# Fifteen output rows of three tiles moved into the last attention body of a streaming encoder layer

## The reference

```
shift, scale, gate = split(silu(c) @ w_ada + b_ada)
h = x * (1 + scale) + shift
qa, ka, va, ga, qb, kb, vb, gb, qi, ki, wi = split(h @ w_in)
oa = banded window attention with sinks and relative bias    (16 heads, 2 key heads)
ob = attention over the top-k keys of an indexer              (16 heads, 2 key heads)
y  = concat(oa * silu(ga), ob * silu(gb)) @ w_out             (2048 x 2048)
x  = LayerNorm(ALPHA * x + gate * y) * ln_g + ln_b
```

## Time and profile before

| | us |
|---|---|
| median of 3 runs | 2007.69 (2005.69 to 2008.35) |
| profiled execution | 2006.17 |
| its span | 2004.4 |
| TensorE busy | 1911.7 (95%) |
| DVE busy | 973.0 (49%) |
| ACT busy | 704.3 (35%) |
| POOL busy | 618.4 (31%) |

### The profile page before, as it was taken

One profiled execution on the slowest core, in us unless ns is written; L12 is line 12 of the kernel. 1 busy time (PEld: TensorE's weight loads), 2 busy tenths in 40 slices (PEclk: granted clock), 3 DMA queues, 4 the chain that ended last, 5 costly groups with the idle time before them and its releaser, 6 DMA issues.

```text
span 2004.4 us, 34267 instructions
## 1 busy us (share of the span) xinstructions
PE 1911.7 (95%) x13047; PEld 1580.4 (79%) x13047; DVE 973.0 (49%) x2360; ACT 704.3 (35%) x1541; POOL 618.4 (31%) x688
## 2 busy tenths in 40 slices
PE   6799999999999999999999999999999889999994
PEld 3367779888888888888888888888887568878773
DVE  2442448856767778874323323323234522226437
ACT  2224332113433343333443434434435622212221
POOL 0331111112222222222333333333323544434552
PEclk8799999999999999999999999999999999999997
DMA  9964112332332332222211111111125154453564
GB/s 342 342 219 137 33 27 69 98 77 75 81 81 63 84 83 77 68 75 64 62 27 44 43 28 44 27 44 44 27 56 174 49 141 133 127 157 116 181 160 121
DMA packets 251267, 195.43 MB, mean 97 GB/s; under 512 B 149969, under 2 KB 203473, under 8 KB 249313
## 3 DMA queue, kind: packets, MB, share of 16 engines
q1 hardware_dynamic: 216560, 160.26, 28.4%
q10 hardware_dynamic: 33472, 28.75, 4.6%
q0 software_dynamic: 1072, 4.24, 0.7%
HBM read 172.86 MB, written 24.53 MB: 98 GB/s over the span
## 4 chain that ended last, share of the span: by engine, by line
PE 83%; DMA 5%; DVE 3%; ACT 3%; POOL 2%; SPq 2%; issue 2%; ACTq 0%; POOLq 0%; DVEq 0%
PE psum L1729 13%; PE psum L1731 12%; PE psum L1730 12%; PE psum L1765 6%; PE psum L1789 6%; PE psum L1809 5%; PE psum L1833 4%; PE psum L1834 4%; PE psum L1835 4%; PE psum L1656 3%; DMA w_raw<-in_w_out_dram 3%; PE psum L1658 3%; PE psum L1657 3%; DMA ada_ring<-in_w_ada_dram 2%; PE psum L1700 2%
## 5 line engine op out<-in xcount | busy, mean ns | idle before, releaser
L1729 PE MATMUL psum<-h_hi,w_hi 128*128 128x364 f32 (+1 forms) x1536 | 521.5, 340 | 5.4 <-issue 3.6
L1731 PE MATMUL psum<-h_lo,w_hi 128*128 128x364 f32 (+1 forms) x1536 | 503.9, 328 | 0.0
L1730 PE MATMUL psum<-h_hi,w_lo 128*128 128x364 f32 (+1 forms) x1536 | 501.8, 327 | 0.0
L1205 POOL TENSOR_TENSOR w_lo<-w_raw,w_hi 128x512 fp32r<-128x512 f32 x128 | 165.1, 1290 | 494.7 <-ACT w_hi L989 494.7
L1729 PEld LDWEIGHTS psum<-h_hi,w_hi 128*128 128x128 f32 x1536 | 289.2, 188 | 14.5 <-issue 11.2
L1730 PEld LDWEIGHTS psum<-h_hi,w_lo 128*128 128x128 f32 x1536 | 289.7, 189 | 0.0
L1731 PEld LDWEIGHTS psum<-h_lo,w_hi 128*128 128x128 f32 x1536 | 288.5, 188 | 0.0
L1043 ACT ACTIVATE w_raw<-psum 128x512 f32<-128x512 f32 (+1 forms) x176 | 95.9, 545 | 497.8 <-PE psum L1789 497.6
L1219 POOL TENSOR_SCALAR room<-room 128x256 f32<-128x256 f32 (+6 forms) x312 | 166.0, 538 | 320.1 <-DVE room L1439 318.1
L1211 POOL TENSOR_TENSOR w_lo<-w_raw,w_hi 128x512 fp32r<-128x512 f32 x120 | 165.7, 1382 | 220.5 <-ACT w_hi L997 220.4
L1833 PE MATMUL psum<-w_hi,h_hi 128*128 128x512 f32 x474 | 188.4, 397 | 5.2 <-POOL w_lo L1211 4.9
(11 more groups left out here) (180 smaller groups left out, 2804.4 us busy)
## 6 DMA issues: line engine op xcount, KB each, us to landing
w_raw<-in_w_out_dram SPq DMA_DIRECT2D x268, 128.0 KB, 2.9
ada_ring<-in_w_ada_dram SPq DMA_DIRECT2D x64, 512.0 KB, 9.7
w_raw<-in_w_in_dram SPq DMA_DIRECT2D x256, 128.0 KB, 2.5
w_raw<-in_w_ada_dram ACTq DMA_DIRECT2D x124, 128.0 KB, 2.2
x_rows<-in_x_prompt_dram SPq DMA_DIRECT2D x8, 1024.0 KB, 12.6
w_raw<-in_w_in_dram SPq DMA_DIRECT2D x32, 256.0 KB, 2.8
room<-in_x_prompt_dram SPq DMA_DIRECT2D x32, 256.0 KB, 5.4
mix_transposed<-room SPq DMA_DIRECT2D x14, 544.0 KB, 3.3
```

Of the source, the lines that this page charges most:

```text
L1729: pe.matmul(Z, w_hi, hh[:, k, a:b], start=(k == 0), stop=False)
L1730: pe.matmul(Z, w_lo, hh[:, k, a:b], start=False, stop=False)
L1731: ins = pe.matmul(Z, w_hi, hl[:, k, a:b], start=False, stop=(k == KT - 1))
```

## The change

- Fifteen of the sixteen rows of a part of three tiles, columns 512 to 1023 of tiles 0 to 2, stand in the last body ahead of the rows of part (0, tiles 0 to 2). `OUT_GAPS` gives them room: 30 rows instead of 16, mostly two a gap. The sixteenth row of each of the two parts comes behind the body.
- The fifteen rows are summed in PSUM banks 0 to 2. ACT then copies the three sums to SBUF (`early_leave`), and the first part uses the same banks. The sixteenth row is summed in another bank later, and `leave` adds the two, one DVE operation more per tile.
- Three raw places in the body: `raw` 0 and two in block 15 of `plain_l`. A load waits for the lo part of the row three before. The first two rows behind the body (31 and 32 in the list) use `raw` 0 alone, each waiting for the lo part of the row before.
- The order of the parts: (0, 0 to 2) and the early one, (3, 0 to 3), the early one's last row (row 47), (2, 0 to 3), (0, 3 to 8), (1, 3 to 8), (2, 4 to 8), (3, 4 to 6), (3, 7 to 8). The number of products is the same.
- Mix blocks start two units earlier (`MIX_ORDER`); block 15 waits on DVE for the lo part of row 29, as its memory holds two raw places.
- Gate rows are loaded at rows 40, 54, 59, 72, 88, 104 and 120 (`GATE_ROW`). `ln_g` and `ln_b` are loaded at row 98, after the end of part (1, 3 to 8), which is row 95. All four normalisations of tiles 0 to 3 follow that part on DVE, and their stores come at rows 104 to 110.

```diff
-OUT_GAPS = [[0, 1], [1], [1], [1], [1, 1], [1, 1], [1, 1], [1, 1], [1, 1], [1, 1], [0]]
+OUT_GAPS = [[0, 1], [2], [2], [2], [1, 2], [1, 2], [2, 2], [2, 2], [2, 2], [2, 2], [1]]
+EARLY = 2
+Y_PARTS = [(0, range(0, 3)), (3, range(0, 4)), (1, range(0, 3)), (2, range(0, 4))] + [(n, range(3, NTILE)) for n in range(2)] \
+    + [(2, range(4, NTILE)), (YN - 1, range(4, 7)), (YN - 1, range(7, NTILE))]
+Y_AMONG = 2 * (KT - 1)
+MIX_ORDER = [[[0], [1]], [[2], [3]], [[4], [5]], [[6]], [[7, 8]], [[9, 10]], [[11], [12]], [[13], [14]], [[], []], [[], []], [[15], []]]
...
+    def out_raw(m):
+        if m < Y_AMONG and m % 3:
+            i = m % 3 - 1
+            return plain_l[:, KT - 1, YC * i:YC * i + YC], early_loaded[i], early_loaded[i].at(32 * (m // 3 + 1))
...
         def load_out(m):
-            if m <= KT:
+            if m == 0:
+                sp.wait_ge(lo_ready.sem, lo_ready.at(NHC + CHUNKS))
+            elif 3 <= m < Y_AMONG:
+                sp.wait_ge(lo_ready.sem, lo_ready.at(NHC + CHUNKS + m - 2))
...
+            elif Y_AMONG < m <= 2 * KT:
                 sp.wait_ge(lo_ready.sem, lo_ready.at(NHC + CHUNKS + m))
...
+        GATE_ROW = [None, 40, 54, 59] + [KT * c + 8 for c in range(YN, 2 * YN)]
+        for m in range(2 * KT + 4, Y_SPLIT):
             load_out(m)
+            if m == KT * (YN + 2) + 2:
+                sp.wait_ge(y_done.sem, y_done.at(Y_AT[YN + 2]))
                 sp.dma_start(lng, row_of(io["ln_g"], 0, D)).then_inc(ln_loaded.sem, 16)
                 sp.dma_start(lnb, row_of(io["ln_b"], 0, D)).then_inc(ln_loaded.sem, 16)
+            for c in range(1, 2 * YN):
+                if m == GATE_ROW[c]:
+                    load_gate(c)
+                if 0 <= m - GATE_ROW[c] - 1 < len(x_tiles(c)):
+                    load_x(c, x_tiles(c)[m - GATE_ROW[c] - 1])
...
+        def early_leave():
+            act.wait_ge(wo_used.sem, wo_used.at(KT - 1))
+            act.wait_ge(mix_lo.sem, mix_lo.at(15))
+            for i in range(len(Y_PARTS[EARLY][1])):
+                act.activation(early_part(i), bank(i), ACT.Copy).then_inc(early_read.sem, 1)
...
+            if c == EARLY:
+                dve.wait_ge(y_done.sem, y_done.at(at_ + 1))
+                dve.tensor_tensor(y, Y, early_part(i).rearrange("p (k n) -> p k n", n=P), ALU.add).then_inc(y_read.sem, 1)
```

More of the change, by code:

```diff
@@ L222, in norm_cuts, with mix_at @@
     return [(0, 4 * P), (4 * P, hi - lo)] if len(turns(u)) == 2 else [(0, hi - lo)]
[L226 to L229, removed]
+MIX_ORDER = [[[0], [1]], [[2], [3]], [[4], [5]], [[6]], [[7, 8]], [[9, 10]], [[11], [12]], [[13], [14]], [[], []], [[], []], [[15], []]]
+def mix_at(u, b):
+    at_ = u - (LAST_BODY - 2)
+    return MIX_ORDER[at_][b] if 0 <= at_ < len(MIX_ORDER) else []
 N_BEFORE = running(2 * len(norm_cuts(u)) for u in range(UNITS))
@@ L512, in build @@
     both_hi = count("both_hi")
+    early_read = count("early_read")
+    early_loaded = [count(f"early_loaded{i}") for i in range(2)]
     both_lo = count("both_lo")
@@ L765, in _ @@
         load_mix(9)
+        mix_room(CHUNKS - 1)
         load_out(1)
[L767 to L770, removed]
         load_out(2)
-        load_mix(13)
-        for q in range(3, KT):
-            load_out(q)
+        for k in range(10, 14):
+            load_mix(k)
+        for m in range(3, 2 * KT + 4):
+            load_out(m)
         def load_gate(c):
@@ L1084, in _ @@
             for b in range(len(gaps(u))):
+                if body == PAIRS - 1 and gap_rows(u, b).start == KT - 1:
+                    early_leave()
                 if u > 0 and b < len(turns(u - 1)):
@@ L1117, in _ @@
                         z_leave(zi, c)
-                if MIX_AT.get((u, b)) is not None:
-                    mix_hi_of(MIX_AT[u, b])
+                for i in mix_at(u, b):
+                    mix_hi_of(i)
             if 0 <= body < 8 and step == 0:
@@ L1141, in _ @@
         mix_hi_of(16)
-        for m in range(KT + 1, Y_SPLIT):
+        for m in range(Y_AMONG + 1, Y_SPLIT):
             hi_out(m)
@@ L1475, in _ @@
                 shift_b(u, 0)
-                if MIX_AT.get((u, 0)) is not None and len(gaps(u)) == 2:
-                    mix_lo_of(MIX_AT[u, 0])
+                if len(gaps(u)) == 2:
+                    for i in mix_at(u, 0):
+                        if i < 15:
+                            mix_lo_of(i)
                 if len(GROUPS[1].s_cuts(u % STEPS)) > 1:
@@ L1481, in _ @@
                 denominator(u, 1)
-                if MIX_AT.get((u, len(gaps(u)) - 1)) is not None:
-                    mix_lo_of(MIX_AT[u, len(gaps(u)) - 1])
+                for i in mix_at(u, len(gaps(u)) - 1):
+                    mix_lo_of(i)
+            if u == UNITS:
+                dve.wait_ge(lo_ready.sem, lo_ready.at(NHC + CHUNKS + Y_AMONG))
+                mix_lo_of(15)
         mix_lo_of(16)
@@ L1544, in _ @@
                 leave(c, i)
[L1545 removed]
+            if c == YN + 1:
                 inverse(0, 4, 3, 1)
[L1547 to L1549 removed]
+                for t in range(4):
+                    normalise(t)
             if c == 2 * YN - 1:
@@ L1818, in out_part @@
             at_ = Y_AT[c] + i
+            place = q - KT * c if c > EARLY else k
+            first, last = place == 0 or q == KT * EARLY + KT - 1, place == KT - 1
+            stop = last or early and k == KT - 2
             w_hi, w_lo = split_place(q)
-            row = y_row(q)
+            row = k
             if i == 0:
```

154 lines of the change are left out of this document (81 added, 73 removed).

## The result

The changed kernel takes 2014.39 us (median of 7 executions, 2005.61 to 2018.93) where the kernel before, on the same chip, takes 2006.95 (2004.77 to 2010.08): 1.003 of its time, with a 95% interval of 1.0017 to 1.0043. So the change costs 5 to 7 us; +6.2 was forecast.

The account below looks back on a forecast made before the run. TensorE was taken to bound the kernel (83% of the chain), with only 19.7 us idle to fill in the last body. -1.1 + 3.0 + 3.5 + 0.8 = +6.2 us gave 2012.4 profiled, 2013.9 median; range 2002 to 2021.

Parts of the forecast that it names:

- start of the body: Start of the last attention body: TensorE's wait for a gated tile stays at 2.5 us.
- second-row waits: Last body, two-row gaps behind transposes: TensorE waits for POOL's rest of the second row, 12 x 0.85 = 10.2 us.
- first rows of a unit: Last body: a unit's first row waits for a rest behind POOL's norms; 0 to 4 us, taken as 1.
- rows 31 and 32: Behind the body: two rows share the single raw place, each waiting for the row before; together 6.4 us, where 2.98 stood.
- slow clock in the body: Last body: half of 3.1 us of slow clock goes as idle stretches get shorter, -1.5 us.
- body in all: Last body and rows behind it: idle after 20.1 less 19.7 before, less 1.5 of clock, -1.1 us; bounds -12 and +4.
- SP's stop at row 59: Tail: SP waits for DVE's three early tiles before the gate row, so load 60 is late; +3.0 us.
- SP's stop at row 98: Tail: the norm's scale and shift wait for row 95's part to end, so row 99's load is late; +3.5 us.
- six tiles in part five: Part five: its last tile needs the fourth read of the part before; 0 to 1.6 us, taken as +0.8.
- Rival A: Tail: loads are early enough, four raw places hide 8 us of SP's standing; no change, 2007.4 us; chance 20%.
- Rival C: Part of row 96: DVE's normalisation passes hold up POOL's rests; 10 us at most, 5 taken, 2019 us; chance 12%.
- Rival B: Last body: filled without the 12 waits, worth 11 us; 2003 us with SP's stops, 1996 without; chance 12%.

Follow-up runs that it names:

- yardstick: The changed kernel itself, unaltered, timed again beside the kernel before on the same chip: median 2013.5 us, 1.0026 of the kernel before.
- all four edits: Changed kernel with gate row at 62, `ln_g`/`ln_b` at 99, first split ahead of score copies, row 31 loaded elsewhere: 1994.89 us, 0.994 of the kernel before.
- the first two edits: Changed kernel with part three's gate row loaded at row 62 and `ln_g`/`ln_b` at 99: 2005.8 and 2005.3 us, 0.9984 and 0.9995 of the kernel before.

## Why the prediction was right, and where it was off

Time and sign came out by the mechanism named. Term by term, against the profile after:

| term | forecast, us | measured |
|---|---|---|
| start of the body | 2.5, stays | 2.46 |
| second-row waits | 12 x 0.85 = 10.2 | nine, 3.9 recorded, 5.4 with overlap |
| first rows of a unit | 1.0 | two, 1.5 recorded, 1.8 with overlap |
| rows 31 and 32 | 6.4 | 3.23 + 1.37 = 4.6 recorded |
| slow clock in the body | -1.5 | nothing won |
| body in all | -1.1 | -2.5 |
| SP's stop at row 59 | +3.0 | wait 3.39 (3.25); time 4.8 |
| SP's stop at row 98 | +3.5 | wait 3.62 (3.83); time 3.7 |
| six tiles in part five | +0.8 | 0.83 |
| all | +6.2 | +7.4 and +5.2 |

**The stops and part five** are the steps that carried the sign, and they were sized from rows of before by counting SP's list against TensorE's rows. As waits they are right to 0.4 us; in time the gate row's stop cost 1.8 more than forecast. Rival A falls, since the two loads were late by just these amounts: a stop is covered for about 5 us, not for 8. With both stops gone the forecast left 2007.4 (rival A's time); 2005.8 and 2005.3 were measured.

**The second-row waits were mis-sized**, the mechanism not. I took 0.85 us from a gap with two transpose copies; the recorded waits run from 0.18 to 0.56, and three of the twelve gaps have none above 0.15. The record of the matmul before a wait ends 0.39 us after its start where the next could begin after 0.227, so each wait is some 0.16 longer than its record: 5.4 + 11 x 0.16 = 7.2. Rows 31 and 32 were overpriced by some 1.5 us. Body and the rows behind it, from the first gated wait to the last row of column block 3 in the part with four tiles, before and after:

```profile
1665.64 0.39 PE L1833 MATMUL psum<-w_hi,h_hi 128*128 128x512 f32 x1
```

```profile
1691.83 0.39 PE L1895 MATMUL psum<-w_hi,h_hi 128*128 128x512 f32 x1
```

The first is row 31 of the kernel before, 129.63 us behind the end of the wait at 1536.01, the second the matching row 46, 157.79 us behind 1534.04: 28.2 us more for 30.7 us of moved products, -2.5 (-2.9 in the yardstick's execution). The stretches up to these rows (columns of the earlier trace rows):

```profile
1531.50:1666.00 134.50, 114.81 (x675) 85.12 (x675) 56.17 (x131) 63.23 (x115) 62.08 (x62) 0.97 0.33 95
```

```profile
1531.50:1692.00 160.50, 147.13 (x782) 107.43 (x781) 54.18 (x129) 68.67 (x126) 78.03 (x74) 0.98 0.38 112
```

Recorded idle time fell by 6.3 us, from 19.7 to 13.4, the time by 2.5. So the forecast's balance, idle time after less idle time before, is in these records good to 4 us and no better; the overlap of four more waits explains 0.6 of that, and the rest isn't placed.

**The clock was on the wrong side.** I took 1.5 us of slow clock as won, since the body's holes get shorter, and priced the two stops at their waits alone. By the two stretches above, 0.97 of 134.5 us and 0.98 of 160.5, the body won nothing or nearly so: behind row 31's hole the clock was lower there. And the change has holes of over 3 us at rows 60 and 99 too, with a lower clock behind each in its two profiled executions. The length alone doesn't bring it: behind the 2.98 us of the earlier trace rows the clock stayed at 1.00 in the kernel before, and so it did behind 3.05 us in the kernel with one raw place:

```profile
1625.00:1630.00 5.00, 5.00 (x24) 4.12 (x23) 0.00 (x0) 1.26 (x2) 1.52 (x3) 1.00 0.83 234
```

```profile
1582.55 0.50 PE L1888 MATMUL psum<-w_hi,h_hi 128*128 128x512 f32 x1 [3.05 <-POOL w_lo L1249]
```

```profile
1582.50:1587.50 5.00, 4.95 (x37) 3.62 (x37) 0.16 (x1) 1.77 (x4) 2.83 (x5) 1.00 0.18 52
```

The same 474 products in three lines (records | busy us, mean ns), before, after and with all four edits:

```profile
L1833 PE MATMUL psum<-w_hi,h_hi 128*128 128x512 f32 x474 | 188.4, 397 | 5.2 <-POOL w_lo L1211 4.9
L1834 PE MATMUL psum<-w_lo,h_hi 128*128 128x512 f32 x474 | 185.7, 392 | 0.0
L1835 PE MATMUL psum<-w_hi,h_lo 128*128 128x512 f32 x474 | 185.6, 391 | 0.0
```

```profile
L1895 PE MATMUL psum<-w_hi,h_hi 128*128 128x512 f32 x474 | 193.1, 407 | 19.1 <-POOL w_lo L1256 18.6
L1896 PE MATMUL psum<-w_lo,h_hi 128*128 128x512 f32 x474 | 188.4, 397 | 0.0
L1897 PE MATMUL psum<-w_hi,h_lo 128*128 128x512 f32 x474 | 188.0, 397 | 0.0
```

```profile
L1902 PE MATMUL psum<-w_hi,h_hi 128*128 128x512 f32 x474 | 188.5, 398 | 5.3 <-POOL w_lo L1262 4.7
L1904 PE MATMUL psum<-w_hi,h_lo 128*128 128x512 f32 x474 | 185.6, 392 | 0.0
L1903 PE MATMUL psum<-w_lo,h_hi 128*128 128x512 f32 x474 | 185.5, 391 | 0.0
```

559.7, 569.5 and 559.6 us: in the profiled execution the products of after carry 9.8 us of longer records, where the yardstick's (565.6 us) carry 5.9. This is a good part of why it is 12.4 us longer in span when 5 to 7 us are typical. From the segments, the wait taken off: 54.64 - 47.99 - 3.39 = 3.3 us behind row 60 and 59.60 - 53.74 - 3.62 = 2.2 behind row 99; in the yardstick's execution 2.0 and, on balance, none (a stretch at 0.66, but without the waits of 0.30 to 0.53 us that the executions without that stop have in this part). So two errors of a few microseconds, the waits too dear and the clock too cheap, cancel; that the sum was right to about a microsecond is partly luck.

**Rival C** didn't come: in the profile after, the longest wait beside the eight normalisation passes is 0.31 us, where the forecast kept 1.14. POOL's rests there are longer, though, and so are DVE's passes:

```profile
1895.80 3.26 DVE L1592 SCALAR_TENSOR_TENSOR room<-room,h_lo_plain 128x2048 f32<-128x2048 f32 x1
1897.46 2.75 POOL L1256 TENSOR_TENSOR w_lo<-w_raw,w_hi 128x512 fp32r<-128x512 f32 x1 [0.55 <-ACT w_hi L1033]
1898.98 3.37 DVE L1590 SCALAR_TENSOR_TENSOR room<-room,h_hi_plain 128x2048 f32<-128x2048 f32 x1
1901.23 2.27 POOL L1256 TENSOR_TENSOR w_lo<-w_raw,w_hi 128x512 fp32r<-128x512 f32 x1 [1.03 <-ACT w_hi L1033]
...
1914.44 1.29 POOL L1256 TENSOR_TENSOR w_lo<-w_raw,w_hi 128x512 fp32r<-128x512 f32 x1 [1.03 <-ACT w_hi L1033]
```

The rests take 2.25 to 2.75 us instead of 1.29, the passes up to 3.38 instead of 2.35. A rest that starts 1.66 or 2.25 us into a pass ends 1.15 us after the pass does, as every rest does that starts under one of these passes, in the kernel before too (1.13 to 1.15): it waits for the pass's end. The two engines do hold each other up for a whole instruction, as the Trainium skill, "SBUF — State Buffer", section "Who interferes with whom", has it. What that costs depends on where in a pass the rest starts: two rests that began 0 and 1.1 us into theirs made the 6.76 us of the earlier trace rows, while here most began over 2 us in and lost about 1 us, within the slack of 1.1 that the forecast counted.

**No term was given** for part (3, tiles 4 to 6), some of whose split rows are kept (`w_kept`) for the last part: TensorE waits 2.34 us there at 1955.56 (1.44 in the yardstick's execution), where the kernel before has 0.99. This and rival C's missing 0.8 us nearly cancel.

**Rival B** had the place right (ACT's order) and the price wrong: it gave 11 us for the second rows' waits, and with all nine gone 3.6 were won. That 1994.89, with row 31 moved as well, is near the 1996 that it gave for a filled body without SP's stops is luck: more than half of what was gained on top of the first two edits is row 31's, which B had left where it was.

## What to carry to other kernels

When a load queue that runs in order gets a wait for another engine, count in rows of the bottleneck engine how far the queue is ahead: stops of 4.6 and 5.3 us were free here, 8.5 cost 3.4 and more, and with one row more ahead of it in the list the stop cost nothing. Moving work into idle time pays only as far as the new work's own feed (split, rest, raw place) is there on time, so look at the order of the feeding engines in the same gap before pricing the fill. Ask how far into another engine's long instruction a short one will start before pricing their conflict. Price a hole of 3 us in TensorE's work at its length and up to as much again.

## What the runs showed of the hardware that I had not expected

Behind the waits of 3.0 to 8.15 us before rows 31, 60 (58) and 99 TensorE's granted clock fell in every profiled execution (in two, behind 3.20 and 3.09 us at row 31, only at row 32's wait), but for a length that differs: after 3.39 us of waiting it was 0.77 and 0.55 in two stretches of 5 us, after 3.62 us 0.63 and 0.69, after 3.83 us 0.66 in one, after 8.15 us 0.50 and 0.79. The matmul's record is then 0.63 us for 0.39, its distance to the next 0.43 for 0.227. Behind waits of up to 1.3 us in the tail (1.26 at 1752, 0.83 at 1815) it stayed at 1.00, and so it did behind 2.98 us in the kernel before and 3.05 in the one with one raw place; behind the 2.46 us at the body's start it fell in most executions (0.69 from 1535 to 1540 in the profile after) and stayed at 1.00 in the one with the gate row at 60. So the length of a wait alone doesn't decide it. The Trainium skill, "TensorE: Matmul & The Clock Gate", Part 1 (on the HAM clock gate), says that a gate passes half the clock's pulses after the engine has been idle; the trace agrees, with 0.50 as the lowest stretch. How much one such wait costs can't be foretold from its length in these runs: 0 to 3.3 us beside the wait itself.
